# Second FFN of a decoder block: GpSimd block sums released by a later count, down passes in another order, residual rows loaded in four quadrants

## The reference, cut to what matters

```python
def swiglu_ffn(h, w_up, w_down):
    gate, up = jnp.split(h @ w_up, 2, axis=-1)
    return (jax.nn.silu(gate) * up) @ w_down
...
        x = x + (g_a * y_a + g_b * y_b) @ w_out[l]

        h = rms_norm(x, norm_ffn2_g[l])
        x = x + FFN_RESIDUAL_SCALE * swiglu_ffn(h, w_ffn2_up[l], w_ffn2_down[l])
    return rms_norm(x, norm_final_g)
```

## Time and profile before

| | us |
|---|---|
| time, median of 3 runs (lowest, highest) | 2315.98 (2314.77, 2318.11) |
| time of the profiled execution | 2315.68 |
| its span | 2313.8 |
| TensorE busy | 2233.2 (97%) |
| VectorE busy | 1639.1 (71%) |
| GpSimd busy | 604.8 (26%) |
| GpSimd waiting for a store of `d_act` | 53.8, in 3 waits |

### The profile page before, as it was taken

One profiled execution on the slowest core, in us unless ns is written; L12 is line 12 of the kernel. 1 busy time (PEld: TensorE's weight loads), 2 busy tenths in 40 slices (PEclk: granted clock), 3 DMA queues, 4 the chain that ended last, 5 costly groups with the idle time before them and its releaser, 6 DMA issues.

```text
span 2313.8 us, 32138 instructions
## 1 busy us (share of the span) xinstructions
PE 2233.2 (97%) x10370; PEld 1839.2 (79%) x10370; DVE 1639.1 (71%) x2145; ACT 954.7 (41%) x1555; POOL 604.8 (26%) x680
## 2 busy tenths in 40 slices
PE   7999999999999999999999899999999999999998
PEld 6788888888788887777787677887877888887886
DVE  5877777655555899999898737653496777765667
ACT  5555555445543122222223122334445555553444
POOL 2888999400000000000000150000333455541000
PEclk9999999999999999999999899999999999999999
DMA  6224444386763234444335432545445566658664
GB/s 167 73 82 133 143 141 139 121 274 194 256 198 123 89 121 151 127 126 136 105 112 180 153 125 78 164 152 185 164 141 180 201 204 204 204 204 299 195 193 173
DMA packets 298523, 370.61 MB, mean 160 GB/s; under 512 B 26457, under 2 KB 198577, under 8 KB 298064
## 3 DMA queue, kind: packets, MB, share of 16 engines
q1 hardware_dynamic: 279376, 300.24, 40.6%
q0 software_dynamic: 19056, 69.42, 8.4%
q10 hardware_dynamic: 16, 0.00, 0.0%
HBM read 259.73 MB, written 107.50 MB: 159 GB/s over the span
## 4 chain that ended last, share of the span: by engine, by line
PE 72%; DVE 19%; issue 4%; DMA 3%; ACT 2%; SPq 1%; POOL 0%; DVEq 0%; ACTq 0%; POOLq 0%
PE PU L1283 10%; PE PU L1285 10%; PE PU L1284 10%; DVE XT L2282 8%; PE PU L1224 5%; PE PU L1226 5%; PE PU L1225 5%; PE PU L1164 3%; PE PU L1163 3%; PE PU L1165 3%; PE PD L1163 3%; PE PD L1164 3%; PE PD L1165 3%; DVE TMP L2360 1%; PE PD L1358 1%
## 5 line engine op out<-in xcount | busy, mean ns | idle before, releaser
L1224 PE MATMUL PU<-Hhi,Whi 128*128 128x512 f32 x896 | 355.6, 397 | 9.8 <-DVE Hlo L2308 6.2
L1226 PE MATMUL PU<-Hhi,Wlo 128*128 128x512 f32 x896 | 351.7, 393 | 0.0
L1225 PE MATMUL PU<-Hlo,Whi 128*128 128x512 f32 x896 | 351.5, 392 | 0.0
L2282 DVE SCALAR_TENSOR_TENSOR XT<-XT,wq 128x1024 f32<-128x1024 f32 x240 | 309.3, 1289 | 7.8
L1043 POOL TENSOR_TENSOR RT<-XT 128x512 f32<-128x512 f32 x2 | 2.9, 1448 | 869.6 <-DMA XT<-d_conv 869.5
L1224 PEld LDWEIGHTS PU<-Hhi,Whi 128*128 128x128 f32 x896 | 170.1, 190 | 49.1 <-DVE Hlo L2308 7.8
L1225 PEld LDWEIGHTS PU<-Hlo,Whi 128*128 128x128 f32 x896 | 170.3, 190 | 35.4 <-issue 0.7
L1226 PEld LDWEIGHTS PU<-Hhi,Wlo 128*128 128x128 f32 x896 | 169.8, 189 | 36.0
L1283 PE MATMUL PU<-Hhi,Dhi 128*128 128x512 f32 x480 | 188.2, 392 | 5.6 <-ACT s1b L1630 5.6
L1285 PE MATMUL PU<-Hhi,Dlo 128*128 128x512 f32 x480 | 187.9, 391 | 0.0
L1284 PE MATMUL PU<-Hlo,Dhi 128*128 128x512 f32 x480 | 187.9, 391 | 0.0
(11 more groups left out here) (401 smaller groups left out, 5268.5 us busy)
## 6 DMA issues: line engine op xcount, KB each, us to landing
d_act<-G SPq DMA_DIRECT2D x88, 256.0 KB, 2.1
XT<-in_w_ffn_down SPq DMA_DIRECT2D x88, 256.0 KB, 3.3
XT<-d_act SPq DMA_DIRECT2D x88, 256.0 KB, 3.5
Wraw<-in_w_ffn_up SPq DMA_DIRECT2D x80, 256.0 KB, 4.5
XT<-in_w_ffn_up SPq DMA_DIRECT2D x80, 256.0 KB, 4.3
Wraw<-in_w_in SPq DMA_DIRECT2D x32, 512.0 KB, 6.0
Wraw<-d_sb SPq DMA_DIRECT2D x55, 256.0 KB, 2.7
TAB<-in_w_ffn_down POOLq DMA_DIRECT2D x11, 1024.0 KB, 5.3
```

Of the source, the lines that this page charges most:

```text
L1224: mm(o_, Whi[s][:, side, k, :], Hhi[:, k, hs[h]], start=k == 0, stop=False)
L1225: mm(o_, Whi[s][:, side, k, :], Hlo[:, k, hs[h]], start=False, stop=False)
L1226: last = mm(o_, Wlo[s][:, side, k, :], Hhi[:, k, hs[h]], start=False, stop=k == KT - 1)
L2282: stt(CVb, z_, w_, CVb, ALU.mult, ALU.add).then_inc(m["conv"], 1)
```

## The change

GpSimd's chain of block sums gets a second wait ahead of its first unit: `u_lo` at 7·(20 + 2), which VectorE's last weight split for pair 1 reaches. Down's passes make product 3 first and product 7 third. Pass 0 then reads raw inner tiles, so its loads wait for `act_saved` and not for `sa_st`; that wait moves to pass 1. The residual is loaded as four quadrants of 1 MB at steps (0, 4), (0, 7), (1, 4) and (2, 4) instead of two halves of 2 MB at (0, 6) and (1, 6), and VectorE's waits for them and ScalarE's first `fin_squares` are moved accordingly.

```diff
-D_ORD = (7, 5, 3, 4, 1, 2, 6)
+D_ORD = (3, 5, 7, 4, 1, 2, 6)
+D_ROWS = ((0, 1), (1, 1), (0, 0), (1, 0))
...
             if p == 0:
+                sp.wait_ge(act_saved[0], 16 * (FT + 2 * t + 1))
+            if p == 1:
                 sp.wait_ge(sa_st, 48 * (t + 1))
...
-        def rows_after_mix(h):
+        ROWS_AT = ((0, 4), (0, 7), (1, 4), (2, 4))
+
+        def rows_after_mix(h, dh):
             sp.wait_ge(x_st, 16 * 2 * J)
             sp.wait_ge(u_prod, 7 * 2 * NSP)
-            load_rows(FFN2, h, d_x2)
+            sp.dma_start(XT[:, 4 * h:4 * h + 4, hs[dh]], d_x2[4 * h:4 * h + 4, :, hs[dh]].rearrange("j c d -> c j d"))\
+                .then_inc(xr_ld, 16)
...
-                if (p, t) in ((0, 6), (1, 6)):
-                    rows_after_mix(p)
+                if (p, t) in ROWS_AT:
+                    rows_after_mix(*D_ROWS[ROWS_AT.index((p, t))])
...
         pool.wait_ge(rd_lo, FFN2.z0)
+        pool.wait_ge(u_lo, 7 * (UBASE[FFN2] + 2))
         weight_sums(0)
...
-                    if (p, t) == (3, 7):
-                        fin_squares(0, 1, 2, 0)
+                    if (p, t) == (2, 7):
+                        fin_squares(0, 1, 1, 0)
...
-                        if t == 2 and p in (1, 3):
-                            dve.wait_ge(xr_ld, {1: 80, 3: 96}[p])
+                        if t == 2 and p in (1, 2, 4):
+                            dve.wait_ge(xr_ld, {1: 96, 2: 112, 4: 128}[p])
```

## The result

The changed kernel takes 2356.44 us as the median of four runs (2345.67 to 2358.7), against 2315.97 for four of the kernel before: the ratio is 1.0165, 95% interval [1.0132, 1.0197]. The prediction said 2345.5, in a range of 2331 to 2356, and a slower kernel. The direction and the cause of the loss are as forecast. The median lies 11 us over the predicted time and 0.4 us over the upper end of the range; by the ratio the time is 2354.2 (1.0165 times 2315.98), just within it. The profiled execution has a span of 2356.3 us, 42.5 more than before's.

A forecast was written before the change was run, and what follows sets the result against it. TensorE, busy 97% of the span, bounds the kernel; GpSimd's slackless block sums gate down. Terms +34.2 - 7.0 + 2.3 = +29.5 us on 2315.68 give 2345.2, or 2345.5 us as a median, range 2331 to 2356.

The forecast's parts named there:

- The chain without slack and the gate: GpSimd's block sums, 19.4 us a unit, never catch up; their delay beyond idle waits holds SyncE's first down load: +34.2 us.
- half the saving for the last two units: Last two block-sum units, run with SyncE's loads silent, could save 3.4 us; half taken, so sums land at 2114.2.
- Down's start: Second FFN's down projection starts at 2120.3 instead of 2086.15, +34.2 us.
- TensorE idles for some 38 us before that: TensorE finishes the up projection, then idles ahead of down's start, so gains at pairs 0 and 1 are worth nothing.
- The 6.1 us from first load to first split: From SyncE's first down load to the end of the split completing step 0: 6.1 us, added to 2114.2.
- the term -7.0 us: Down's pass 0: new order and 1 MB loads remove the 4.66 us stall and 2.3 us of slow clock after it.
- the second rival: Down's first pass is crowded: a 4.66 us stall and 2.3 us of slow clock return, giving 2352.5 us; 13%.
- - 7.0 + 2.3: Down's first pass: -7.0 us for the removed stall and slow clock, +2.3 us for a slow start after the long idle.
- called them hidden: Last inner tile's stores, queued behind SyncE's wait, cost nothing: their sums are needed only near 2177, later than 2133 + 20.
- Pairs 0 to 2: Up projection: silent GpSimd shortens three VectorE instructions by 3.6 us, removing up to 3.9 us of TensorE's stalls.
- the two stalls I named: TensorE's stalls of 1.27 and 2.59 us at up's pairs 0 and 1, blamed on VectorE slowed by GpSimd's additions.
- The sums catch up: Rival: block-sum units run at 17.7 us, down is ready at 2084.3, and the kernel gets faster, 2307 us; 5%.

## Why the prediction was right, and where it was not

**The chain without slack and the gate: right.** The step read from the earlier trace rows, that what GpSimd's start is moved by beyond its idle waits comes out at SyncE's first load for down, carries the result. Taking the wait out takes the loss away; the wait alone makes all of it. The numbers: sums begin at 1726.79 (forecast 1724.2), weight sums landed by 2112.14 (2114.2), 19.3 us a unit. Of the forecast's choices, half the saving for the last two units: the two that begin at 2077.64 and 2094.86 took 17.2 and 17.3 us, so all of it came. The Trainium skill, DMA: Bandwidth & Descriptors, section Latency and other measured facts, has a DMA's fixed cost fall with a lighter load on the memory. The traces agree for these units: the waits for the stores from 2077.64 on were 2.40, 2.32 and 2.40 us with SyncE's loads silent, and 6.40, 6.00 and 2.40 us where down's loads ran beside them (a wait per step). A light load is not the only way to such waits: with the latest start they were 2.3 to 2.4 us beside the pairs' loads too (last section).

**Down's start: 2125.14 instead of 2120.3, and the step that failed is "TensorE idles for some 38 us before that".** I had it idle behind pair 19, for 30 to 45 us ahead of its first PD matmul; the 39.36 us lie within pair 19. ScalarE and VectorE execute their queues in order, and down's first splits stand among pair 19's combinations; so TensorE stopped two products early, and made these 24 matmuls, 12 of them at a granted clock of 0.50, only when the gate was open. The 6.1 us from first load to first split came out as 2115.71 + 0.69 - 2111.55 = 4.9, but 8.7 us of pair 19 followed. Moving the splits confirms it.

**Down's first pass: the term -7.0 us failed, and the second rival's stall came.** The stalls of pass 0 add up to 7.8 us of idle (0.47, 1.30, 5.06, 0.99), with a slow clock after the longest, where I had said no stall of 4 us. I had put 13% on a crowded pass and 0 us in the sum. From down's start to the span's end the changed kernel takes 231.2 us and the kernel before 227.7: the term measures +3.5 us, not -7.0. The rest of the gap to the forecast is here, since for this stretch the forecast had 2313.8 - 2086.15 - 7.0 + 2.3 = 223. With 4.8 us from down's start that makes the 13 us between the forecast span of 2343.3 and 2356.3.

What I overlooked stands in SyncE's queue. I had the last inner tile's stores behind the gate and called them hidden, since only sums needed them; but down's own loads from step 4 on stand behind these stores, which wait for pair 19's combinations. So the stop in pair 19 comes back in pass 0: SyncE waited 10.9 and 5.0 us for two of these combinations and issued step 4's loads 7.4 us after down's start, where it was 2.8 us in the kernel before, and then the quadrants, 4.3 us apart. The runs with quadrants at steps 4 and 7 fall in two groups. Where pair 19 is stopped (the changed kernel in both profiles, the wait behind two units, the wait two pairs later) step 4's loads come 6.6 to 7.4 us after down's start, and pass 0 idles for 5.6 to 7.8 us. Where it isn't (the wait taken out, the wait behind two units with the wait per step, and the splits moved behind) they come 0 to 2.9 us after it, and it idles for 2.3 to 4.3 us (up to 4.5 with the first steps of pass 1). The means of the groups are 6.3 and 3.8 us, so an estimate of 2.5 us comes from the late loads and not from the crowd. It is read from the traces and was not tried alone; the groups also differ in how far the quadrants lie apart and in which units run beside them.

The other part is the residual. The new order makes pass 1 add into two quadrants, so both must be loaded in pass 0: 2 MB as before, only in two pieces. I had counted these 2 MB, but held the cut into 1 MB loads to be enough. The old order needs one quadrant there, and has 1.31 us of stall. That the lengthened splits of VectorE, up to 2.45 us in pass 0, have a share is not shown: the version with later quadrants has splits of 2.44 us in pass 0 and no stall.

**Pairs 0 to 2: the cause was right for the most part, the reading of the rows was not.** The lengthened VectorE instructions are gone: none of 128x512 took over 0.7 us between 1700 and 1724. Idle at the pairs fell from 6.4 us in four places to 3.04 us in one, where I had up to 3.9 us less. Of the two stalls I named, the first is gone, and the second stays at 3.04 us: it wasn't GpSimd's. The one at pair 1's product 7 (2.00 us) went instead; I had left it out, and called 1.27 us one of the two largest. As forecast, it is worth nothing while the gate holds; in the versions without the gate it is worth at most the 4 us seen in medians.

**The sums catch up: refuted,** at the start put by the change. The unit's mean would have had to be 18.0 us. It was 19.3, and 18.7 with the latest start tried.

## What to carry to other kernels

An engine that is busy 26% of the time can have no slack at all, if its work is a chain of load, compute and store through one buffer: count the units and the time of one, and look only for waits that are not its own transfers. Delay such a chain by what its idle waits absorb and no more, and let the consumer wait for the piece it needs, not for all. Work of the next stage that is queued ahead of the last work of this one saves time while its data is early, and holds up this stage when it is late; a store of this stage's last result that is queued ahead of the next stage's loads then holds up these as well.

## What the runs showed of the hardware that was not expected

The duration of a block-sum unit depends on where it lies between other transfers. With the start at 1756.98 the waits ahead of the 20 loads that follow were 2.3 to 2.4 us at 17 of them, and the units took 18.7 us on the mean. With the start at 1726.79 these waits were 2.2 to 5.6 us and the mean was 19.3. This rests on one profile of the later start. Two units of 18.7 us are shorter than two pairs of TensorE (38.1 us), two of 19.3 are longer; it is the same work. That the weight loads of the pairs are what meets the stores in one case and not in the other is a guess, and was not tried.

In the changed kernel a 128x512 tensor_tensor of VectorE with both inputs in SBUF took up to 2.50 us beside GpSimd's additions; those with one input in PSUM took 0.67 to 0.69 us, each of the 239 that the timeline lists singly from 1550 us on. The Trainium skill, SBUF — State Buffer, section SBUF: two separate sides, says that VectorE with two inputs in SBUF and GpSimd reading SBUF share a pair of ports, which one of them holds for a whole instruction. The trace agrees, with the two numbers above.

A pass of down ran without a stall at a DMA share of 0.96 (354 GB/s, later quadrants), and one at 0.88 (320 GB/s, the changed kernel) stood still for 7.8 us. The share of a stretch does not tell whether the loads that its steps need come in time.
